# A hybrid attention and expert-retrieval step on one core: three more waits, and cheaper empty steps, in the cost table that places a front's steps

## The reference, cut to what matters

```python
h = rms(x) @ w_in                      # split into q, latent, keys, gates ...
x = x + (sigmoid(ga) * (o_a @ w_o_a) + sigmoid(gb) * (o_b @ w_o_b)) @ w_out
...
v1, i1 = lax.top_k(s1, PEER_TOPK)      # 16 of 128, two halves, 8 heads
v2, i2 = lax.top_k(s2, PEER_TOPK)
e = i1_of_chosen * N_KEYS + i2_of_chosen
g = jax.nn.softmax(sc, axis=-1)
a = jax.nn.gelu(jnp.einsum('td,thkd->thk', t, u[e]))
out = jnp.einsum('thk,thkd->td', g * a, v[e])
```

## Time and profile before

| | us |
|---|---|
| median of 3 runs | 1798.29 |
| the three runs | 1796.89, 1798.29, 1798.40 |
| the profiled execution | 1796.99 |
| its span in the trace | 1795.2 |

### The profile page before, as it was taken

One profiled execution on the slowest core, in us unless ns is written; L12 is line 12 of the kernel. 1 busy time (PEld: TensorE's weight loads), 2 busy tenths in 40 slices (PEclk: granted clock), 3 DMA queues, 4 the chain that ended last, 5 costly groups with the idle time before them and its releaser, 6 DMA issues.

```text
span 1795.2 us, 26399 instructions
## 1 busy us (share of the span) xinstructions
PE 1223.4 (68%) x9056; PEld 679.3 (38%) x9056; DVE 1310.8 (73%) x3857; ACT 579.7 (32%) x1995; POOL 526.2 (29%) x569
## 2 busy tenths in 40 slices
PE   8989976677867575878877666679867343434343
PEld 3668532344535232444535223356535111111111
DVE  5662696989666676989666768998766878686754
ACT  2331134333423333334323334344423222222222
POOL 0200232333322223332322223232323333333332
PEclk9989889787988696897998697887999555555555
DMA  6238699999999999999999999999999999999997
GB/s 267 74 100 294 250 422 421 422 425 425 424 424 423 417 401 383 420 425 424 425 423 422 423 407 390 426 400 398 422 424 423 427 426 426 425 427 423 427 421 294
DMA packets 119381, 696.48 MB, mean 388 GB/s; under 512 B 17983, under 2 KB 21118, under 8 KB 49102
## 3 DMA queue, kind: packets, MB, share of 16 engines
q0 software_dynamic: 78848, 570.53, 76.0%
q1 hardware_dynamic: 36686, 121.83, 17.5%
q10 hardware_dynamic: 3712, 2.43, 0.4%
HBM read 691.65 MB, written 3.02 MB: 387 GB/s over the span
## 4 chain that ended last, share of the span: by engine, by line
DMA 35%; DVE 25%; PE 25%; issue 6%; ACT 3%; POOL 1%; ACTq 0%; DVEq 0%; SPq 0%; POOLq 0%
DMA rows<-in_peer_uv,index 26%; DVE rows L2657 11%; PE ps_v L1820 5%; DMA wch<-in_w_row 4%; PE ps_f L1559 4%; PE ps_f L1353 2%; PE ps_f L1574 2%; PE ps_h L1800 2%; DMA wch<-in_peer_wq 2%; DVE score L2333 1%; PE ps_f L1477 1%; PE ps_f L1653 1%; DVE best L2332 1%; DMA wch<-in_w_ukv 1%; PE ps_f L1437 1%
## 5 line engine op out<-in xcount | busy, mean ns | idle before, releaser
L2657 DVE CUSTOM_DVE_ANT_0 rows<-rows,ps_h 128x1024 f32<-128x1024 f32 x544 | 658.0, 1220 | 289.1 <-DMA rows<-in_peer_uv,index 236.3
L1330 POOL DMA_INDIRECT rows<-in_peer_uv,index x544 | 516.4, 949 | 1169.4 <-PE ps_v L1820 988.8
L1820 PE MATMUL ps_v<-rows,diag 128*32 128x256 f32 x4352 | 419.1, 500 | 432.0 <-ACT diag L2164 424.8
L1820 PEld LDWEIGHTS ps_v<-rows,diag 128*32 128x32 f32 x4352 | 124.2, 130 | 677.5 <-ACT diag L2164 561.7
L2155 ACT ACTIVATE tan<-arg 128x2 f32<-128x2 f32 x272 | 55.3, 203 | 799.2 <-DVE arg L2667 756.4
L2158 ACT ACTIVATE weight<-tan,lead 128x1 f32<-128x1 f32 x544 | 180.8, 379 | 9.1
L2164 ACT ACTIVATE diag<-sel,weight 128x32 f32<-128x32 f32 x544 | 140.9, 306 | 0.6 <-PE ps_v L1820 0.6
L1559 PEld LDWEIGHTS ps_f<-bufh,wch 128*128 128x128 f32 x768 | 103.7, 214 | 19.9 <-issue 17.8
L1559 PE MATMUL ps_f<-bufh,wch 128*128 128x128 f32 x768 | 109.7, 302 | 0.0
L1353 PE MATMUL ps_f<-wch,bufh 128*128 128x512 f32 (+1 forms) x192 | 81.9, 565 | 27.7 <-DMA wch<-in_w_row 26.7
L1653 PE MATMUL ps_f<-bufh,wch 128*128 128x128 f32 x384 | 52.1, 293 | 12.5 <-DMA wch<-in_peer_wq 12.3
(11 more groups left out here) (398 smaller groups left out, 1682.4 us busy)
## 6 DMA issues: line engine op xcount, KB each, us to landing
wch<-in_w_gate SPq DMA_DIRECT2D x60, 512.0 KB
wch<-in_w_row SPq DMA_DIRECT2D x36, 512.0 KB
wch<-in_w_o SPq DMA_DIRECT2D x32, 512.0 KB
wch<-in_w_out SPq DMA_DIRECT2D x24, 512.0 KB
wch<-in_peer_wq SPq DMA_DIRECT2D x24, 512.0 KB
rows<-in_peer_uv,index POOLq DMA_INDIRECT x544
w_tok<-in_w_tok SPq DMA_DIRECT2D x4, 1640.0 KB, 12.9
wch<-in_w_uq SPq DMA_DIRECT2D x6, 384.0 KB
```

Of the source, the lines that this page charges most:

```text
L1330: pool.indirect_dma_start(rows[c % RING][:, :, :].rearrange("p a d -> p (a d)"), None, io.peer_uv[:, :], at).then_inc(s_uv[c % RING], 16)
L1820: ins = nc.tensor.matmul(ps_v[GROUP * a:GROUP * (a + 1), :], diag[:, c % DRING, :], rows[c % RING][:, 1, QD * a:QD * (a + 1)], start=False ...
L2657: v.tensor_tensor_reduce(out=u, in0=u, in1=ps_h[:, :], scale=1.0, scalar=0.0, op0=ALU.mult, op1=ALU.add, accum_out=dots[:, c % KEEP:c % KE ...
```

## The change

Two numbers of the cost table are added and one is lowered. `SOME = 1.5` and the existing `HANDS = 2.4` stand for a wait that is now counted at three steps: x = 5 (turn of x), x = 17 (copies of queries and keys) and k = `at.rows` (turn of the rows). The empty steps ahead of a front (x < 2, six steps, only for p > 1) count 0.5 and no longer 1.5. The instructions are the same ones; only the columns at which they stand change.

```diff
+SOME = 1.5
...
     pe_head = {5: DC * small, 8: 7 * small, 13: 3 * small, 16: 4 * 0.67 + 2 * wide, 23: 9 * small, 26: 2 * H * small, 27: HANDS}
+    pe_head.update({5: DC * small + SOME, 17: HANDS})
     pe_head.update({x: 4 * wide for x in range(7, 13) if x != 8})
...
-        pe, dve = (pe_head.get(x, 0), dve_head.get(x, 1.5 if x < 2 and p > 1 else 0)) if k < 0 else (0, 0)
+        pe, dve = (pe_head.get(x, 0), dve_head.get(x, 0.5 if x < 2 and p > 1 else 0)) if k < 0 else (0, 0)
...
+        if k == at.rows:
+            pe += SOME
```

## The result

| | before | after |
|---|---|---|
| median of 14 runs, us | 1798.04 | 1805.51 |
| lowest and highest, us | 1792.37, 1801.08 | 1799.29, 1808.28 |
| the profiled execution, us | 1796.99 | 1802.12 |
| its span, us | 1795.2 | 1800.0 |

The ratio after / before is 1.0042, with a 95% interval from 1.0029 to 1.0054: the changed kernel is slower by some 7.5 us. The forecast was 1803.5, in a range from 1794 to 1810. The profiled execution lay in the lower part of after's runs, and its trace shows 4.8 us of the 7.5.

The account below looks back on a forecast made before the run. The prediction took the DMA engines as the bound. Its terms, +8.0 for x_sum and -2.8 given back, made +5.2 us on 1796.99, so 1802.2, and 1803.5 for the median, in a range from 1794 to 1810.

Parts of the forecast that it names:

- Bytes fixed, rate varies: Whole kernel: bytes stay the same, so time changes only by how long the DMA engines run below full rate.
- x_sum: Starts of p = 2 and 3: DVE waits longer for x, gathers stop; +4.5 and +3.5, sum +8.0 us (+4 to +14).
- a sign of being wrong: One listed sign: x_sum waits long, but the windows there (near 620 and 1020) stay where they were.
- Fixed cost of a DMA: Gaps at both starts: about 2.0 us more per gather issued into an empty queue, +12 not +8; used only for upper end.
- Copies of queries and keys: After up: DVE waited 7.08 us; one dot of 1.22 us fills the wait in p = 2, worth 0.
- What the columns give back: Last projection to turn of the heads, p = 2 and 3: three added columns return 0.95 us each, -2.8 (0 to -9.4).
- Turn of the heads and first scores: Around spread: some 3 us off PE's path, 1 to 2 us put on it; taken as 0, from -2 to +1.
- Turn of the rows and p = 1: No window near either shows a loss and steps move by one column; 0, from -0.5 to +1 us.
- The rest of p = 2 and 3: One column earlier against choice of experts and block ends; losses at 1160 and 1240 shrink or grow: 0, -3 to +3.
- No change: Rival: the queue carries the gap and the stretch behind gives it all back; 1796 to 1800, chance 0.28.
- The placing does what its numbers say: Rival: extra columns fill both stretches and the two later windows close; -5.9 us, 1792.4, chance 0.12.
- The delay goes on: Rival: projection and its weights start late, both queues run dry; +14 and nothing back, 1812, chance 0.10.

Follow-up runs that it names:

- x_sum_alone: Against before, DVE calls x_sum at column 2 and not 4 in p = 2 and 3, every other step unmoved; 1805.93 us, 1.0041.
- up_to_heads: Against before, only steps x = 16 to 29 (up to first scores) of p = 2 and 3 stand at after's columns; 1803.14 us, 1.0006.
- only_p1: Against before, the new numbers are used for the front of p = 1 alone; 1798.69 us, 0.9994.
- waits_only: Against after, the empty steps keep 1.5, so only the three added waits are counted; 1806.14 us, 1.0031 against before.
- start_only: Against before, only the steps ahead of up (x < 16) of p = 2 and 3 stand at after's columns; 1801.07 us, 1.0012.
- after_x_early: Against after, x_sum and x_scale of p = 2 and 3 read a second copy of x, loaded early into xin; 1803.84 us, 1.0027 against before.
- early_copy: Against before, p = 2 and 3 load x early into xin, ACT copies it to xb, steps ahead of k = 2 at after's columns; 1795.96 us, 0.9980.

## Why the prediction was right, point by point

- **Bytes fixed, rate varies.** Right. 696.47 MB after, 696.48 before, and the time follows where the DMA runs below 425 GB/s.
- **x_sum, +8.0 (4.5 and 3.5).** The mechanism was right: DVE's wait grew to 6.40 and 7.32 us where 7.6 and 8.1 were forecast, and the gathers stopped for 11.9 and 13.3 us, with 13.1 and 13.6 forecast. Alone it costs +7.95 us by the medians, with an interval from 4 to 11. Two points of the working were off. PE's new order, `turn_x` ahead of two mixes, isn't needed for the gap, as x_sum_alone shows. And the margin that I gave p = 3 isn't there: its start lost 0.0 before and 4.0 to 5.9 us in all five kernels with the early wait, above the 3.5. At p = 2 the trace of after misleads. It shows 0.4 us more than before, and its window at 620 stayed (363, then 358), which by my own list was a sign of being wrong. But the window was under 380 before the change, so that sign could hardly tell, and in this execution DVE waited 6.40 us where it waited 7.2 to 7.7 in the four other kernels with the early wait. Those lost 6.5 to 8.8 us there, 3.2 to 5.5 over before, about the 4.5 forecast (0.3 to 5.2 in the nine kernels without the wait).
- **Fixed cost of a DMA.** x_sum_alone, which holds the early wait and no other move, came to +7.95 us, and its interval ends at 11. In its trace the rate at the start of p = 3 fell to 57 GB/s in one microsecond, so the queue ran nearly dry. The Trainium skill, page "DMA: Bandwidth & Descriptors", section "Anatomy of one DMA — SWDGE (gpsimd) path", counts some 2 us for a DMA beside its bytes, by which this term would have been +12: not borne out here, though no run isolated that cost.
- **Copies of queries and keys, 0.** The wait shrank by 4.4 us (7.08 to 2.68). That this is worth nothing is consistent with up_to_heads (1.0006), which moves these steps, though it moves others too.
- **What the columns give back, -2.8.** Right in direction and too small. In the two traces the block ends lost 5.0 and 5.7 us before, and 2.0 and 1.0 after: -7.7. The weak step is the price of 0.95 us for a column, which counted the added columns only. x_sum_alone adds none and still lost 0.9 and 4.1 less there. My reading is that what a delay ahead has cost is partly returned where DVE, and not the DMA, sets the pace; no run tests that reason. up_to_heads, which takes columns away from this stretch in p = 3 and adds none in p = 2, shows no gain.
- **Turn of the heads and first scores, 0.** The wait for the spread stayed at 5.63 us, and no run shows a change from it.
- **Turn of the rows and p = 1, 0.** only_p1 came to 0.9994. In the trace of after, columns 0 to 128 lost 3.3 us more than before, but only 0.6 to 0.9 more in the three other kernels with the same columns in p = 1, so most of the 3.3 belongs to the execution and not to the change. The working was wrong in a detail: it said that no window near shows a loss, but the window from 220 to 240 of before ran at 386 GB/s (384 after).
- **The rest of p = 2 and 3, 0 (-3 to +3).** This is the term that was mis-sized the other way. From before to after the rest of p = 2 lost 1.9 us more and the attention of p = 3 2.3 more, 4.2 in all and above the +3. waits_only, with no early wait at all, is 6.3 us slower than before, and after is some 5.4 slower than start_only. The pair after_x_early and early_copy says the same: neither has the early wait, they differ by the steps from k = 2 on, by those of p = 1, by the way x gets into `xb` and by the 2.5 us of added bytes, and their ratios are 0.47% apart, 8.5 us, so about 6 us without the bytes (3 to 9 by the intervals). Which steps cost it stays open.

So the sum came out near the truth with two errors in it that offset each other: the give-back was larger than -2.8, and what I had put at 0 cost something. In the one pair of traces the starts and block ends together are 3.0 us better after than before (0.4 + 4.3 - 3.0 - 4.7). The +4.8 of the span stands in pass 1 (+3.3), the rest of p = 2 (+1.9), the attention of p = 3 (+2.3), and the stretch ahead of the first column (+1.1), less 1.0 behind column 352 and that 3.0 (to within 0.2 of rounding). That the early wait costs time rests on x_sum_alone, and on the starts, which lose 4.0 us and more at p = 3 in every kernel that has it and 0.3 or less in every kernel without, not on that pair.

- **The rivals.** "No change" said that the queue would carry the gap. It didn't at p = 3 (422, then 330 GB/s at 1020), and 1805.5 lies outside its 1796 to 1800. "The placing does what its numbers say" was to be decided by block ends at 420 or more with the wait for the copies gone; they came close (397 to 421), and yet the two later windows didn't close (411 and 370). Without the wait for x, the part ahead of k = 2 does pay: early_copy. "The delay goes on" to 1812 didn't happen; the block ends stopped it.

## What to carry to other kernels

In a kernel whose engines all run one woven order, first ask of each step what it waits for and when that can arrive. A step placed ahead of that moment makes its whole engine stand still, and with it everything that feeds the bound resource. Two columns too early for one instruction cost 8 us here (4 to 11), about as much as the whole change. A wait that is long because of a buffer is removed by another buffer, not by counting it: loading x some 19 us ahead of its use into a free tile, with the front's steps up to the first scores placed earlier, gained 4.1 us, of which the early load by itself accounts for 1.9 by the medians (within the noise) and the placing for 2.2. And where many small moves come together, time them apart; a sum that is right can hold wrong terms.

## What the runs showed of the hardware

- A load of 0.52 MB on SP's queue, with gathers of 1.05 MB queued, took 7.7 us from issue to use in p = 2 of after and 8.3 before. At 425 GB/s its own bytes take 1.2. A second load of the same size, issued at the end of the pass before, cost nothing that shows at the starts (after_x_early: 1.1 and 0.0 us lost there).
- A pause of POOL of some 7.3 us was carried without a loss at the start of p = 3 (before: 425 GB/s over that stage); with one of 12.3 us the stage lost 4.4 us (after). In x_sum_alone the rate held for some 11 us after the last gather's issue and then fell to 57 GB/s.
- The spread between executions differs from program to program. before ran from 1793.7 to 1807.5 us in 35 runs, and early_copy, run beside it, from 1794.1 to 1797.1 in 12. Its lowest time is no lower than before's; what it gained is that it is nearly always there.
